# Layer 0's queries of heads 2 to 7 for two heads at once, from half-row blocks, turned and scored a slot or two later

## What is computed

```python
def peer_ffn(xn, w_query, subkeys, u_tbl, v_tbl):
    ...
        q = (xc @ w_query).reshape(C, PEER_HEADS, 2, PEER_KEY_DIM)
        s = jnp.einsum('chpd,hpnd->chpn', q, subkeys).astype(jnp.float32)
        s1, i1 = lax.top_k(s[:, :, 0], PEER_TOPK)
        s2, i2 = lax.top_k(s[:, :, 1], PEER_TOPK)
        cand = (s1[..., :, None] + s2[..., None, :]).reshape(C, PEER_HEADS, PEER_TOPK * PEER_TOPK)
        top_s, top_c = lax.top_k(cand, PEER_TOPK)
        idx = (jnp.take_along_axis(i1, top_c // PEER_TOPK, axis=-1) * PEER_N_KEYS
               + jnp.take_along_axis(i2, top_c % PEER_TOPK, axis=-1))
        gate = jax.nn.softmax(top_s, axis=-1)
        act = jax.nn.gelu(jnp.einsum('chkd,cd->chk', u_tbl[idx], xc).astype(jnp.float32), approximate=False)
        coef = (gate * act).astype(xc.dtype)
        return jnp.einsum('chk,chkd->cd', coef, v_tbl[idx])
```

## Time and profile before

| | |
|---|---|
| median of 3 runs | 1555.82 us |
| the profiled execution | 1556.29 us |
| its span, first to last instruction | 1554.4 us |
| TensorE busy | 1301.9 us, 84% |
| VectorE busy | 1035.5 us, 67% |
| GpSimd busy | 981.4 us, 63% |
| ScalarE busy | 404.2 us, 26% |
| DMA | 607.55 MB, mean 391 GB/s |
| gathers (queue 0) | 536.94 MB, 87.4% of 16 engines |
| weights (queue 1) | 69.73 MB, 12.7% |

### The profile page before, as it was taken

How to read it: one execution, slowest core, us unless ns; L and a number is a source line. 1 busy time by engine, 2 the same in 40 slices (tenths; PEclk the granted TensorE clock), 3 DMA queues, 4 the chain that set the end, 5 groups by cost and what they waited for, 6 DMA issues and landing times.

```text
span 1554.4 us, 13400 instructions
## 1 busy us (share of the span) xinstructions
PE 1301.9 (84%) x4046; PEld 688.4 (44%) x4046; DVE 1035.5 (67%) x2464; ACT 404.2 (26%) x877; POOL 981.4 (63%) x1038
## 2 busy tenths in 40 slices
PE   9999888898679888867987889989889797667776
PEld 8996544444335443323433444444434343222232
DVE  3367577766777476637666747476777776776765
ACT  1121322222222324223321232333222322112222
POOL 0066477777676656656576665566657777777773
PEclk9999999989889999878988899999999898788888
DMA  9699999999999999999999999999999999999996
GB/s 331 198 344 361 397 402 409 405 404 407 409 409 405 392 403 406 402 403 408 405 397 404 397 401 399 406 399 409 362 405 409 409 410 409 410 410 409 410 409 269
DMA packets 197708, 607.55 MB, mean 391 GB/s; under 512 B 17597, under 2 KB 50437, under 8 KB 197637
## 3 DMA queue, kind: packets, MB, share of 16 engines
q0 software_dynamic: 147456, 536.94, 87.4%
q1 hardware_dynamic: 50048, 69.73, 12.7%
q10 hardware_dynamic: 132, 0.04, 0.0%
HBM read 605.59 MB, written 1.05 MB: 390 GB/s over the span
## 4 chain that ended last, share of the span: by engine, by line
PE 50%; DMA 23%; DVE 10%; issue 6%; POOL 6%; ACT 4%; DVEq 0%; ACTq 0%; POOLq 0%
PE sums L937 31%; DMA rows<-in_peer_u,expert 15%; DVE rows L1815 7%; DMA rows<-in_peer_v,expert 7%; POOL rows L669 6%; PE banks L769 5%; PE banks L778 5%; PE banks L785 4%; DVE h L1806 2%; DMA wring<-in_attn_w_q 2%; ACT soft_diag L1335 1%; PE sums L778 1%; ACT L1325 1%; PE sums L949 1%; DVE coef L1834 0%
## 5 line engine op out<-in xcount | busy, mean ns | idle before, releaser
L937 PE MATMUL sums<-rows,soft_diag 128*128 128x512 f32 x1764 | 865.3, 652 | 211.6 <-ACT soft_diag L1335 211.4
L1815 DVE SCALAR_TENSOR_TENSOR rows<-rows,xn_near 128x1024 f32<-128x1024 f32 x512 | 604.3, 1216 | 227.7 <-DMA rows<-in_peer_u,expert 222.8
L669 POOL DMA_INDIRECT rows<-in_peer_v,expert x512 | 495.3, 967 | 316.9 <-PE sums L937 165.2
L937 PEld LDWEIGHTS sums<-rows,soft_diag 128*128 128x128 f32 x1764 | 364.7, 210 | 686.9 <-issue 430.3
L669 POOL DMA_INDIRECT rows<-in_peer_u,expert x512 | 484.0, 945 | 235.7 <-issue 140.2
L1335 ACT ACTIVATE soft_diag<-ident,coef 128x128 f32<-128x128 f32 x446 | 161.5, 396 | 238.3 <-DMA rows<-in_peer_v,expert 197.6
L1325 ACT ACTIVATE gelu<-dots 128x8 f32<-128x8 f32 (+1 forms) x65 | 13.5, 207 | 352.1 <-DVE rows L1815 350.1
L1806 DVE SCALAR_TENSOR_TENSOR h<-rows,coef,h 128x1024 f32<-128x1024 f32 x63 | 80.6, 1280 | 0.0
L1269 ACT ACTIVATE scores<-banks 128x512 f32<-128x512 f32 (+1 forms) x52 | 25.5, 493 | 179.5 <-PE banks L807 62.6
L1877 DVE SCALAR_TENSOR_TENSOR soft_diag<-banks,soft_diag 128x512 f32<-128x512 f32 (+1 forms) x8 | 7.7, 958 | 82.3 <-ACT soft_diag L1360 82.3
L785 PE MATMUL banks<-wring,xT 128*128 128x512 f32 x128 | 57.0, 595 | 0.0
(11 more groups left out here) (230 smaller groups left out, 1007.6 us busy)
## 6 DMA issues: line engine op xcount, KB each, us to landing
wring<-in_w_kv SPq DMA_DIRECT2D x14, 1024.0 KB, 16.1
rows<-in_peer_u,expert POOLq DMA_INDIRECT x512, 11.8
rows<-in_peer_v,expert POOLq DMA_INDIRECT x512, 11.8
wkept<-in_peer_w_query SPq DMA_DIRECT2D x8, 1024.0 KB, 16.4
rows<-in_conv_w_in SPq DMA_DIRECT2D x7, 1024.0 KB, 12.5
wring<-in_peer_w_query SPq DMA_DIRECT2D x7, 1024.0 KB, 13.5
wring<-in_attn_w_q SPq DMA_DIRECT2D x7, 1024.0 KB, 17.0
wkept<-in_conv_w_out SPq DMA_DIRECT2D x4, 1024.0 KB, 12.3
```

Source lines behind the costliest of these rows:

```text
L669: nc.gpsimd.indirect_dma_start(row[j], None, table, bass.IndirectOffsetOnAxis(ap=expert[n % 2][:, k:k + 1], axis=0)).then_inc(landed[j], 16)
L937: last = nc.tensor.matmul(sums[:, half, :], diag[:, k % GROUP, :], v_row[k % V_SLOTS][:, half * 512:(half + 1) * 512], start=(first and k ...
L1815: nc.vector.scalar_tensor_tensor(out=u_row[j], in0=u_row[j], scalar=1.0, in1=xn_near[:, :, :].rearrange("p a d -> p (a d)"), op0=ALU.mult, ...
```

## The change

The six blocks of weights of heads 2 to 7 become two half blocks for each pair of heads: 4 x 128 rows of 2 KB in place of 8 x 128 rows of 1 KB, in the same places and order. A pair's query is eight products of 512 columns into a whole bank. Tables `MADE`, `TURNED` and `SCORED` give for each pair the slot in which it is made, turned and scored. Chunk 1 has four pairs; its first takes the blocks of heads 0 and 1. The last scores are read at the head of slot 16, so `mixer_slot` has no queries of layer 0. ScalarE reads what TensorE made in a slot one slot later, made and turned queries behind that slot's `weigh` and scores ahead of it, but for pair (0, 1) in slot 1 and the turned tiles in slot 5. The output projection moves from slots 1 and 2 to 2 and 3, its addition from step 1 to step 2, chunk 1's norm to the end of slot 5, its turn to slot 6. A key block of layer 1 now waits for the pair of slot 8, and the next two blocks in the ring for that of slot 10.

```diff
--- before.py
+++ after.py
@@ -119,38 +119,33 @@
     fill("act", 2, "query", 0, 0, 1)
     fill("act", 3, "score", 0, 0, 1)
 
-    AT_ONCE = (0, 2)
-    ASKED = {2: (0, 3), 4: (0, 4), 5: (1, 0), 6: (0, 5), 7: (1, 1), 8: (0, 6), 9: (1, 2), 10: (0, 7),
-             11: (1, 3), 13: (1, 4), 15: (1, 5)}
-    LAST_ASKED = [(1, 6), (1, 7)]
-    QUERY_SLOT = {asked: i % 2 for i, asked in enumerate([AT_ONCE] + [ASKED[t] for t in sorted(ASKED)] + LAST_ASKED)}
+    MADE = {1: (0, 1), 4: (0, 2), 6: (0, 3), 8: (1, 0), 10: (1, 1), 12: (1, 2), 13: (1, 3)}
+    TURNED = {1: (0, 1), 5: (0, 2), 7: (0, 3), 9: (1, 0), 11: (1, 1), 13: (1, 2), 14: (1, 3)}
+    SCORED = {1: (0, 1), 5: (0, 2), 8: (0, 3), 10: (1, 0), 12: (1, 1), 14: (1, 2), 15: (1, 3)}
+    ASKED_SLOT = {asked: i % 2 for i, asked in enumerate(MADE.values())}
+    OUT_AT = {2: 0, 3: 1}
...
@@ -302,8 +294,11 @@
     for q in range(NB):
         stream_whole(conv_w_out[0], q * COLS, ("out0", q // 2), "out0", q)
     stream_whole(peer_subkeys[0], None, ("subkeys", 0, 3), "subkeys", 0)
-    for hd in range(HEADS):
-        stream_whole(peer_w_query[0], hd * COLS, ("query", 0, 1, hd), "query", 0, hd)
+    for hd in range(2):
+        stream_whole(peer_w_query[0], hd * COLS, ("pair0", 1, 0), "query", 0, hd)
+    for i in range(1, HEADS // 2):
+        for kh in range(2):
+            stream(peer_w_query[0], (kh * KT // 2, KT // 2), 2 * i * COLS, ("bank", FILL["pair0", 1, i]), "query", 0, i, kh)
 
...
@@ -461,7 +456,7 @@
         spare = soft_diag[:, 2 * GROUP * P:]
         notlog = spare[:, 0:8 * P].rearrange("p (e k) -> p e k", e=2)
 
-        queryT = soft[:, :, 0:2 * P].rearrange("p b (s t) -> p b s t", t=P)
+        asked_rows = [soft[:, b, :] for b in range(2)]
         kvT, mixT = xT[:, :, 0:P], xT[:, :, P:T]
 
...
 
-            def query(layer, c, hd):
-                if (c, hd) == (1, 1):
+            def second_query():
...
+            def asked(c, i):
+
+                bank, xt = take("pair0", c, i), xT[:, :, c * P:(c + 1) * P]
+                if i == 0:
+                    to_tokens(bank[:, 0:COLS], weights_of("query", 0, 0), xt)
                     pe.wait_ge(query_moved, 1)
-                    w = w_place[MOVED_TO]
+                    last = to_tokens(bank[:, COLS:2 * COLS], w_place[MOVED_TO], xt)
                 else:
-                    w = weights_of("query", layer, hd)
-                if (c, hd) == (0, 1):
-                    to_features(take("query", layer, c, hd), w, xT[:, :, c * P:(c + 1) * P], P)
-                else:
-                    to_rows(w, xT[:, :, c * P:(c + 1) * P], "query", layer, c, hd)
-
...
+            def score_asked(c, i):
+
+                wait_read(pe, "turned", "pair0", c, i)
+                bank = take("scored0", c, i)
+                for r in range(4):
+                    last = nc.tensor.matmul(bank[:, r * P:(r + 1) * P], asked_tiles(c, i)[:, r, :], subT[:, 4 * i + r, :],
+                                            start=True, stop=True)
                 last.then_inc(bank_done, 1)
 
...
@@ -1030,18 +1039,9 @@
             def mixer_slot(c, t):
 
                 if t == 0:
-                    if c == 0:
-                        score(0, *ASKED[SLOTS - 1])
-                        for asked in LAST_ASKED:
-                            query(0, *asked)
-                        for asked in LAST_ASKED:
-                            turn_query(*asked)
                     transpose_norm("kv", c)
                 if t == 1:
                     wait_read(pe, "turn", "kv", c, 1)
-                    if c == 0:
-                        for asked in LAST_ASKED:
-                            score(0, *asked)
                     to_rows(weights_of("key", c, 0), kvT, "key", c, 0)
                     to_rows(weights_of("qry", c, 0), mixT, "qry", c, 0)
                     turn_key(c, 0)
@@ -1191,35 +1191,35 @@
                 if j == LATER[1]:
                     transpose_subkeys(0, [2, 3])
                 conv_group(1, j)
-            query(0, 0, 1)
-            score(0, 0, 1)
+            second_query()
+            second_score()
 
 
             for t in range(SLOTS):
                 combine(t // GROUPS, (t // GROUPS) % 2, t % GROUPS)
-                if t - 1 in ASKED:
-                    score(0, *ASKED[t - 1])
-                if t == 5:
+                score_first = t in SCORED and TURNED.get(t) != SCORED[t]
+                if score_first:
+                    score_asked(*SCORED[t])
+                if t in TURNED and MADE.get(t) != TURNED[t]:
+                    turn_asked(*TURNED[t])
+                if t == 8:
                     wait_read(pe, "turn", "ffn0", 1, 1)
-                if t in ASKED:
-                    query(0, *ASKED[t])
-                    if t != 2:
-                        turn_query(*ASKED[t])
+                if t in MADE:
+                    asked(*MADE[t])
+                if t in TURNED and MADE.get(t) == TURNED[t]:
+                    turn_asked(*TURNED[t])
+                if t in SCORED and not score_first:
+                    score_asked(*SCORED[t])
                 if t == 0:
                     conv_group(1, LATER[3])
-                if t == 1:
-                    query(0, *AT_ONCE)
-                    turn_query(*AT_ONCE)
-                    score(0, *AT_ONCE)
-                if t in (1, 2):
+                if t in OUT_AT:
                     wait_read(pe, "conv", 1, LATER[-1], 0)
-                    out_half(1, t - 1)
-                if t == 2:
-                    turn_query(*ASKED[t])
+                    out_half(1, OUT_AT[t])
+                if t == 3:
                     pe.wait_ge(gains_loaded, 16 * 3)
                     for half in range(2):
                         spread_half(take("gain0", half), 8, half).then_inc(bank_done, 1)
-                if t == 4:
+                if t == 6:
                     transpose_norm("ffn0", 1)
 
...
+            def asked_made(c, i):
+
+                slot = ASKED_SLOT[c, i]
+                if scored_in_slot[slot]:
+                    wait_filled(act, "scored0", *scored_in_slot[slot])
+                scored_in_slot[slot] = (c, i)
+                read(("pair0", c, i), asked_at(c, i))
+
+            def asked_turned(c, i):
+                read(("turned", "pair0", c, i), asked_at(c, i))
+
+            def asked_scored(c, i):
+
                 if c == 0:
                     act.wait_ge(normed, normed_count("ffn0", 0))
-                read(("score", layer, c, hd), score_at(c, hd), lambda bank: bank[:, 0:2 * KEYS],
-                     scale=1.0 if c else stat[:, 4, 0:1])
+                at = c * HEADS + 2 * i
+                read(("scored0", c, i), scores[:, at:at + 2, :].rearrange("p a k -> p (a k)"), scale=1.0 if c else stat[:, 4, 0:1])
 
...
+            second_query()
+            second_score()
             move_query()
             wait_read(act, "conv", 1, LATER[1], 1)
             conv_group(1, LATER[3])
             for t in range(SLOTS):
                 n, g = t // GROUPS, t % GROUPS
+                if t - 1 in SCORED:
+                    asked_scored(*SCORED[t - 1])
                 if t > 0:
                     weigh(n, n % 2, g)
                 if g == 0:
                     gates(n + 1, 1 - n % 2)
+                if t - 1 in TURNED and t - 1 not in (1, 5):
+                    asked_turned(*TURNED[t - 1])
+                if t - 1 in MADE and t - 1 != 1:
+                    asked_made(*MADE[t - 1])
+                if t == 1:
+                    asked_made(*MADE[t])
+                if t in (1, 5):
+                    asked_turned(*TURNED[t])
+                if t == 4:
+                    first_gain_made()
+                    act.wait_ge(dot_done, TOPK)
+                    wait_input(act, "ffn0", 1)
+                    nc.scalar.activation(xn[:, :], h[:, 1, :], ACT.Square, accum_out=stat[:, 0, 1:2]).then_inc(squares, 1)
                 if t == 5:
+                    nc.scalar.preload_act_table_set("natural_log_exp_and_others")
+                    estimate("ffn0", 1)
+                if t == 7:
                     turned_norm("ffn0", 1, xT[:, :, P:T])
-                if t == 3:
-                    first_gain_made()
-                    nc.scalar.preload_act_table_set("natural_log_exp_and_others")
-                    act.wait_ge(dot_done, TOPK)
-                    norm_sums("ffn0", 1)
-                if t - 1 in ASKED:
-                    scored(0, *ASKED[t - 1])
-                if t in ASKED:
-                    queries(0, *ASKED[t])
...
                 for t in range(SLOTS):
                     n = HEADS * (1 + c) + t // GROUPS
-                    if c == 1 and t == 0:
-                        pair_scored(0, 1)
+                    if t == 0:
+                        if c == 0:
+                            asked_scored(*SCORED[SLOTS - 1])
+                        else:
+                            pair_scored(0, 1)
...
@@ -1896,8 +1898,6 @@
                 if t == 0:
```

(72 more changed lines are left out.)

69 lines of the change are left out of this document (25 added, 44 removed).

## The result

The changed kernel takes 1560.62 us, the median of 10 runs (1557.24 to 1561.97), against 1556.24 for the kernel before (10 runs): a ratio of 1.0026, 95% interval 1.0018 to 1.0034. That is 4.4 us slower, where 1554.0 was forecast in a range up to 1558.5. The profiled execution, the slowest of the ten, has a span of 1560.0 us against 1554.4, 5.6 more.

What follows compares the result with a forecast made beforehand. Full DMA engines bound the kernel; 1.2 us (wider weight rows) and 0.7 us (dip at 500 to 510) off 1556.29 gave 1554.4, or 1553.9 against the median, written 1554.0; own range 1552.7 to 1555.6, 8-in-10 range 1550.0 to 1558.5.

Steps and rivals of the forecast that it cites:

- The norm of chunk 1: Moved from slot 3 to 5, some 3 us of VectorE; its TensorE turn to slot 6; nothing in the total.
- a share under 1.00 between 200 and 500: Sign of being wrong: DMA share under 1.00 anywhere from 200 to 500 us.
- the slower rival: Slots 6 to 13: pairs' heavy slots run into each other on a colder TensorE clock; about 1559.5 us, chance 0.11.
- VectorE's 9.4 us of the earlier trace: VectorE's stall for the output projection before coefficients; it goes, but was covered at full DMA share, so worth zero.
- the 4 us that the prediction named as a sign of being wrong: Slots 12 to 15: GpSimd standing over 4 us for TensorE's sums would show the prediction wrong.
- a landing time of 8.1 us: Gathers' issue-to-landing time at which the DMA share fell, down from 11.8 us; lateness costs from 3.7 us on.
- The weight blocks: Six blocks in 2 KB rows, 2.64 us a MB against 2.84, all while engines are full: 1.2 us gained.
- the estimate from the fixed cost of a packet: Weight blocks: some 3 cycles a packet, so 0.13 us a block and 0.8 us in all; not used for the total.
- Slot 1: First pair needs both half blocks; TensorE waits at worst 3.2 us, combination 2 isn't late: zero.
- Slots 16 and 17: Layer 0's queries, turns and scores leave; combination 17 starts some 1.7 us earlier and the DMA share's dip mostly closes.
- The 0.7 us: Gain from closing the DMA share's dip to 0.96 at 500 to 510 us; ends 0 and 1.1.
- The sum: Whole kernel: 1.2 and 0.7 us off the profiled execution, set against the runs' median: 1553.9, written 1554.0.

## Why the prediction was wrong

**The norm of chunk 1** is the step that failed. The prediction priced it at "some 3 us of VectorE" and put nothing for it into the sum. It counted the instructions, not the order they stand in on ScalarE: the estimate is queued behind a copy that waits for TensorE's turn, which stands behind a whole combination. It named who waits for every moved weight block and not who waits for the moved estimate. The wait was 18.3 us, where up to 12.9 was free, and the DMA engines were dry for some 5.2 us; with the estimate moved ahead of the copy the wait was 8.7 us and the time 5.5 us less. Its own list of what would show it wrong had the sign, a share under 1.00 between 200 and 500, but no rival carried it; the slower rival sat in slots 6 to 13. The prediction called VectorE's 9.4 us of the earlier trace rows covered by four weight blocks in flight. No run took such blocks away there, but in slot 5, with none in flight from 226 to 258, 8.7 and 12.9 us of wait were free too, so a wait of that size does not need them.

**The slower rival** (heavy slots run into each other) did not decide. Slots 12 and 13 with their pairs took 43.4 us from combination to combination (383.42 to 426.83), where the rival's sum had 44.5, and the share over 264 to 500 was 1.03. GpSimd stood 8.0 us for TensorE's sums in slots 12 to 15, over the 4 us that the prediction named as a sign of being wrong, but it had stood 6.5 us there before, both times at a full share; the sign could not tell the cases apart. Nor is a landing time of 8.1 us the point at which the share falls. From 220 to 286 in the kernel before, where the earlier trace rows has 1.03:

```profile
rows<-in_peer_v,expert POOLq DMA_INDIRECT x29, 7.8
```

TensorE's busy time fell by 19.7 us, 14.3 of it in the combinations, and none of it reached the end, which agrees with reading the DMA engines as the bound.

**The weight blocks.** Their price a MB was right. In the changed kernel from 170 to 205, columns as in the earlier trace rows:

```profile
q1 hardware_dynamic: 1360, 2.72, 20.6%
```

0.206 x 35 / 2.72 is 2.65 us a MB, where 2.64 was taken from the earlier trace rows. Narrow again in pairs 2 and 3 alone, with the engines full, four blocks cost 1.5 us by the medians and 2.0 by the means, each uncertain by about 1; 0.8 was expected, so the run does not contradict the price and does not pin it down. What the estimate from the fixed cost of a packet gave, 0.5 us for four (the Trainium skill, "DMA: Bandwidth & Descriptors", section "Why small descriptors are slow (HBM only)"), lies in the same band and can't be told from it. For the two blocks of pair 1 no run shows what their bytes alone are worth: they are issued from 127.9 on, where the engines were not all full (0.83 from 120 to 134.5 after the change, 0.88 before), and the loss by the late second block hides the rest. There the wide form is what lets the pair stand in slot 1.

**Slot 1.** "At worst it waits 3.2 us ... combination at 161 isn't late either way" was half right. The wide blocks did land some microseconds earlier:

```profile
DMA to landing us min/median/max: 12.0/13.9/15.8
```

131.5 + 15.8 = 147.3, ahead of TensorE's 150.4, combination 2 started at 158.9, and the 9.4 us stall of the earlier trace rows was gone. But "either way" was wrong: a wait of 3.2 us was called harmless, and with narrow rows waits of 2.98 and 4.08 us moved combination 2 to 164.4 and 166.3 and cost 6 us. The step overlooked the same thing as at the norm, ScalarE's read of the scores standing ahead of the gelu.

**Slots 16 and 17.** Combination 17 came 491.88 - 468.65 = 23.2 us behind combination 16, against 24.96 before:

```profile
468.65 15.23 PE L946 MATMUL sums<-rows,soft_diag 128*128 128x512 f32 x28 [6.57 <-ACT soft_diag L1344]
...
491.88 13.88 PE L946 MATMUL sums<-rows,soft_diag 128*128 128x512 f32 x28 [7.12 <-ACT soft_diag L1344]
```

1.7 us closer, as worked out. What had stood in the way is gone: VectorE waits 0.28 us for the gelu there, where it had waited 2.05. The share from 500 to 510 is 1.03 here and with the estimate behind `weigh`, but 1.00 with the estimate in slot 4. The 0.7 us never showed in the time, in the kernel that does this alone.

**The sum.** Without the hole the kernel takes 1555.07 and 1555.17, 1.2 us under the kernel before, where 1.9 was forecast. That this equals the 1.2 us put down for the bytes is not shown to be more than chance, as the runs with narrow rows give no such clean split.

## What to carry to other kernels

When a step that two engines hand back and forth is moved, list for each engine what stands ahead of it in its new place, down to the instruction that its neighbour is itself waiting for; a step of 0.4 us behind the wrong copy made VectorE wait 18.3 us here, and 8.7 ahead of it. Then follow the wait to the engine that issues the transfers: up to 5.2 us of GpSimd's standing was free in three kernels, and at 9.7 the time rose. And ask of a shorter transfer not only what its bytes cost but whose first use it meets: the same narrow rows cost 1.5 to 2 us in four blocks with time to spare and 6 in two without.

## What the runs showed of the hardware

A block of 1 MB in 1 KB rows takes much longer to get through beside gathers than its price says: the second of the two blocks landed 21.9 us after its issue with all six narrow, and 15.8 us after it with wide rows (the changed kernel), at prices that differ by some 0.2 us a block. With pair 1 alone narrow it was 23.0 us, and with the estimate in slot 4 and all wide 15.5. In the profile's count a packet of the weights is one row, of 1 KB (2119 for 2.14 MB) or 2 KB (1360 for 2.72 MB). If the weights and the gathers take turns on the DMA engines, the block with more bytes in a packet gets through sooner; that is an inference. The Trainium skill ("DMA: Bandwidth & Descriptors", section "Queues, rings and completion order") says that the engines go round their queues a packet at a time, and the landing times agree with it; the turns themselves were not measured.
